# Another order for the head of a transformer-layer kernel: x turned by token tiles, and half of chunk 0 of the modulation behind four tiles of x

## What is computed

```python
c_act = silu(c)
mod = (c_act @ w_ada + b_ada)                  # 6144 columns: 12 chunks of 512
sh_m, sc_m, g_m, sh_f, sc_f, g_f = split(mod, 6)
u = layer_norm(x) * (1 + sc_m) + sh_m          # needs chunks 0, 1 (shift) and 2, 3 (scale)
z = u @ w_in                                   # 5120 columns: blocks of 128
# ... then pooling, chunked attention, a convolution, gates, projections,
# layer_norm, and an MLP (squared ReLU) with a second layer_norm
```

## Time and profile before

| | us |
|---|---|
| median of 3 runs | 1433.06 (1431.15 to 1433.45) |
| the profiled execution | 1431.08 |
| its span in the profile | 1429.3 |
| first matmul of the projections | 44.69 |
| first matmul of queries, keys and values | 122.37 |

### The profile page before, as it was taken

The page is one execution under the profiler, slowest core; times in us unless marked ns, Lnnn a source line. Parts: engine busy times, 40 slices in busy tenths (PEclk is TensorE's granted clock), DMA queues, the critical chain, the costliest instruction groups (busy, mean ns, idle before and its releaser), DMA issues.

```text
span 1429.3 us, 17335 instructions
## 1 busy us (share of the span) xinstructions
PE 1401.4 (98%) x6554; PEld 1150.8 (81%) x6554; DVE 965.6 (68%) x1334; ACT 634.6 (44%) x902; POOL 420.1 (29%) x453
## 2 busy tenths in 40 slices
PE   6999999999999999999999999999999999999996
PEld 1788788888878888888888888888888888888885
DVE  3877677776579955365668797565665746447687
ACT  3412577787541224111616774433445535343251
POOL 1005356556556000000024317434444200001215
PEclk9999999999999999999999999999999999999998
DMA  9883454665565322762632455444445978466361
GB/s 347 276 292 120 133 171 154 184 182 159 162 218 171 112 90 77 245 191 90 199 126 89 160 181 195 143 146 155 162 155 207 302 257 301 169 222 235 111 228 59
DMA packets 159035, 256.42 MB, mean 179 GB/s; under 512 B 11304, under 2 KB 81374, under 8 KB 158952
## 3 DMA queue, kind: packets, MB, share of 16 engines
q1 hardware_dynamic: 144104, 204.97, 42.9%
q0 software_dynamic: 14848, 50.34, 10.5%
HBM read 182.36 MB, written 68.71 MB: 176 GB/s over the span
## 4 chain that ended last, share of the span: by engine, by line
PE 83%; DVE 9%; DMA 2%; ACT 2%; issue 2%; SPq 1%; POOL 0%; DVEq 0%; ACTq 0%; POOLq 0%
PE ps L1977 22%; PE ps L1979 22%; PE ps L1978 22%; PE ps L2105 10%; PE ps L2145 2%; PE ps L2155 2%; PE ps L2170 2%; DVE bn L1330 1%; DMA mid<-in_x_dram 1%; DVE mid L1710 1%; DMA t_raw<-u_scratch 1%; DVE part_lo L1834 1%; DVE partial L1381 1%; DVE mix_tmp L1703 1%; PE ps L2044 1%
## 5 line engine op out<-in xcount | busy, mean ns | idle before, releaser
L1977 PE MATMUL ps<-act_hi,w_hi 128*128 128x512 f32 (+1 forms) x496 | 192.6, 388 | 0.4 <-DVE w_lo L1841 0.4
L1979 PE MATMUL ps<-act_hi,w_lo 128*128 128x512 f32 (+1 forms) x496 | 190.2, 384 | 0.0
L1978 PE MATMUL ps<-act_lo,w_hi 128*128 128x512 f32 (+1 forms) x496 | 190.0, 383 | 0.0
L1834 DVE TENSOR_TENSOR part_lo<-k_raw,part_hi 128x1024 fp32r<-128x1024 f32 x112 | 146.5, 1338 | 56.1 <-ACT part_hi L897 53.4
L1978 PE MATMUL ps<-part_lo,part_hi 128*128 128x512 f32 x448 | 174.3, 389 | 0.0
L1977 PE MATMUL ps<-part_hi 128*128 128x512 f32 x448 | 174.3, 389 | 0.0
L1979 PE MATMUL ps<-part_hi,part_lo 128*128 128x512 f32 x448 | 174.3, 389 | 0.0
L897 ACT ACTIVATE part_hi<-k_raw 128x1024 fp32r<-128x1024 f32 x112 | 116.4, 1059 | 110.6 <-DMA k_raw<-tw_scratch 48.9
L1324 DVE TENSOR_TENSOR w_lo<-w_raw,w_hi 128x1024 fp32r<-128x1024 f32 x52 | 68.5, 1316 | 68.4 <-ACT w_hi L897 68.3
L1977 PEld LDWEIGHTS ps<-act_hi,w_hi 128*128 128x128 f32 x496 | 93.4, 188 | 19.2 <-issue 0.7
L1978 PEld LDWEIGHTS ps<-act_lo,w_hi 128*128 128x128 f32 x496 | 93.5, 188 | 18.5 <-issue 1.0
(11 more groups left out here) (249 smaller groups left out, 3168.7 us busy)
## 6 DMA issues: line engine op xcount, KB each, us to landing
k_raw<-h_scratch SPq DMA_DIRECT2D x112, 256.0 KB, 4.5
ada<-in_w_ada_dram SPq DMA_DIRECT2D x11, 2048.0 KB, 9.4
w_raw<-in_w_in_dram SPq DMA_DIRECT2D x42, 512.0 KB, 4.5
tw_rows<-in_w_ff_dram POOLq DMA_DIRECT2D x64, 256.0 KB, 4.1
tw_scratch<-tw_sum POOLq DMA_DIRECT2D x32, 512.0 KB, 3.4
h_scratch<-h_sum POOLq DMA_DIRECT2D x64, 256.0 KB, 2.8
k_raw<-tw_scratch SPq DMA_DIRECT2D x64, 256.0 KB, 5.5
pair_raw<-in_w_ff_dram SPq DMA_DIRECT2D x13, 1024.0 KB, 6.1
```

The costliest lines, as they stand in the source:

```text
L1834: nc.vector.tensor_tensor(part_lo[s][:, :, :], k_raw[rs][:, :, :], f(part_hi[s][:, :, :]), ALU.subtract)\
L1977: nc.tensor.matmul(out, sh, mh, start=first, stop=False)
L1978: nc.tensor.matmul(out, sh, ml, start=False, stop=False)
L1979: return nc.tensor.matmul(out, sl, mh, start=False, stop=last)
```

## The change

The head is written anew up to the end of block 5; behind it nothing but the numbering of semaphores differs (some are merged, and the last tile's normalisation has one of its own).

- **Loads.** Chunk 0 comes in two halves with x tiles 0 to 3 between them, chunk 2 in two halves with tiles 4 and 5 between, then tiles 6 and 7, block 0, chunk 1, block 1, chunk 3, block 2 (waiting for `cut_lo(0)`), the biases, chunk 4 (waiting for DVE's chunk 1), block 3, and so on.
- **Chunk 1** goes from TensorE to DVE (`N_DIRECT` 2). Its columns are made by `row_columns(1)` out of `partial`.
- **Transposes** go by token tiles: eight transposes of one tile as soon as it is normalised, between the half chunks on TensorE. ACT copies each turned tile from PSUM to a new buffer `x_t` in SBUF (DVE the last one). ACT's modulation then reads `x_t`, and no longer waits for transposes.
- **act_hi** is cut by ACT instead of DVE, step 0 apart.
- **Products.** The steps of blocks 0, 1 and 2 are interleaved, with a third pair of buffers for block 2 in the place of normalised x. First steps 0 to 3 of blocks 0 and 1, then half of chunk 3, then steps 0 to 3 of block 2, then the columns of chunks 1 and 3, and then steps 4 to 7 of the three blocks. Blocks 3, 4 and 5 follow whole.

```diff
-N_DIRECT = 3
+N_DIRECT = 2
...
+            load_ada_half(0, 0)
+            load_x(range(4))
+            load_ada_half(0, 1)
...
+            load_ada_half(2, 0)
+            load_x(range(4, 6))
+            load_ada_half(2, 1)
+            load_x(range(6, ST))
+            load_block(0)
             load_ada(1)
-            load_x(range(5, ST))
-            load_block(0)
+            load_block(1)
             load_ada(3)
-            load_block(1)
...
+            def modulate_x(k):
                 if k >= 2:
                     act.wait_ge(u_lo_done, k - 1)
-                act.wait_ge(z_done, k + 1)
-                nc.scalar.activation(u_tmp[k % 2][:, :], banks(2 * (k % 2)), ACT.Identity, bias=mod[:, k:k + 1],
-                                     scale=mod[:, KT + k:KT + k + 1]).then_inc(u_tmp_done, 1)
+                nc.scalar.activation(u_tmp[k % 2][:, :], x_t[:, k, :], ACT.Identity, bias=mod[:, k:k + 1],
+                                     scale=mod[:, KT + k:KT + k + 1]).then_inc(u_step, 1)
+                if k >= 1:
+                    act.wait_ge(u_step, 2 * k)
+                    copy(act_hi[:, k, :], u_tmp[k % 2][:, :]).then_inc(u_step, 1)
...
+            act.wait_ge(mod_done, 1)
+            act.wait_ge(x_copied, ST)
+            for k in range(3):
+                modulate_x(k)
+            cut_hi(1)
+            modulate_x(3)
+            cut_hi(2)
+            save_ada_row(3)
+            act.wait_ge(mod_done, 2)
+            for k in range(4, KT):
+                modulate_x(k)
...
+            mixer_columns(0)
+            dve.wait_ge(z_done, ST)
+            nc.vector.tensor_copy(x_t[:, :, (ST - 1) * P:ST * P], tile_banks(ST - 1)).then_inc(x_copied, 1)
+            cut_lo(0)
+            cut_u_lo(0)
+            cut_u_lo(1)
+            cut_lo(1)
+            cut_u_lo(2)
+            start_chunk(1)
+            cut_u_lo(3)
+            end_chunk(1)
+            cut_lo(2)
+            ada_chunk(3)
+            mixer_columns(1)
+            cut_u_lo(4)
+            start_chunk(4)
+            for k in range(5, KT):
+                cut_u_lo(k)
+            end_chunk(4)
+            cut_lo(3)
...
             pe.wait_ge(head_sb_done, 2)
+            row_chunk(0, 0)
+            transpose_x(0)
+            transpose_x(1)
+            row_chunk(0, 1).then_inc(head_ps_done, 1)
+            transpose_x(2)
+            transpose_x(3)
...
+            row_chunk(2, 0)
+            transpose_x(4)
             row_columns(0)
+            transpose_x(5)
+            row_chunk(2, 1).then_inc(head_ps_done, 1)
+            transpose_x(6)
             row_columns(2)
+            transpose_x(7)
...
+            pe.wait_ge(w_lo_done, 1)
+            for k in range(2):
+                rows_part(0, k)
+            pe.wait_ge(w_lo_done, 2)
+            for k in range(2):
+                rows_part(1, k)
+            for n in range(2):
+                for k in range(2, 4):
+                    rows_part(n, k)
+            pe.wait_ge(mod_done, 1)
+            row_chunk(3, 0).then_inc(head_ps_done, 1)
+            pe.wait_ge(w_lo_done, 3)
+            for k in range(4):
+                rows_part(2, k)
+            row_columns(1)
+            row_columns(3)
+            for k in range(4, 6):
+                for n in (1, 0, 2):
+                    rows_part(n, k)
+            for n in (1, 0, 2):
+                for k in range(6, KT):
+                    rows_part(n, k)
```

More of the change, by code:

```diff
@@ L94, in trunk_layer @@
     act_lo = at("act_lo", [P, KT, SEQ], f32r, 32 * KB)
+    x_t = at("x_t", [P, KT, SEQ], f32, 32 * KB)
     mid = at("mid", [P, KT, SEQ], f32, 64 * KB)
@@ L338, in block_used @@
             if n < N_P1:
-                return z_done, 8 + n + 1
+                return z_done, ST + P1_END[n]
             if n < N_G:
@@ L920, in save_ada_row, with save_tile @@
             def save_ada_row(i):
-                act.wait_ge(head_ps_done, (1, 5, 4, 6)[i])
+                act.wait_ge(head_ps_done, {0: 1, 2: 4, 3: 5}[i])
                 copy(ada_row[i], ps[0:1, ADA_BANKS[i], :]).then_inc(head_sb_done, 1)
[L924 to L928, removed]
+            def save_tile(i):
+                act.wait_ge(z_done, i + 1)
+                copy(x_t[:, :, i * P:(i + 1) * P], tile_banks(i)).then_inc(x_copied, 1)
@@ L929, in _ @@
+            for i in range(0, ST, 2):
+                take_root(i, i)
+                take_root(i + 1, i + 1)
+                norm(i, i, mid[:, i, :])
+                if i + 1 < ST - 1:
+                    norm(i + 1, i + 1, mid[:, i + 1, :])
                 if i == 2:
                     save_ada_row(0)
-                elif i == 4:
+                if i == ST - 2:
                     save_ada_row(2)
[L933 to L941, removed]
+                    cut_hi(0)
+                    save_tile(i)
+                else:
+                    save_tile(i)
+                    save_tile(i + 1)
@@ new lines, in _ @@
+            act.wait_ge(mod_done, 1)
[9 more added lines that the diff above has]
+                modulate_x(k)
+            cut_hi(3)
+            for n in (0, 2, 3, 4, 5):
+                act.wait_ge(z_done, ST + P1_END[n])
+                src = banks(P1_BANKS[n])
@@ L1345, in _ @@
             dve.wait_ge(head_sb_done, 2)
[L1346 to L1351, removed]
+            for i in range(0, ST, 2):
+                for t in (i, i + 1):
+                    dve.wait_ge(x_in[t], 16)
+                    stats(mid[:, t, :], t)
+                for t in (i, i + 1):
+                    scale_bias(t, t)
+                if i == 4:
+                    dve.wait_ge(head_ps_done, 3)
+                    nc.vector.tensor_copy(cols[:, 0:ROWS_A], ps[:, 7, PIECE:PIECE + ROWS_A])
+                    nc.vector.tensor_copy(cols[:, ROWS_A:ROWS_A + ROWS_C], ps[:, 7, PIECE + P:PIECE + P + ROWS_C])\
+                        .then_inc(cols_done, 1)
             dve.wait_ge(norm_ready, ST)
             nc.vector.tensor_scalar(mid[:, ST - 1, :], mid[:, ST - 1, :], rstd[:, ST - 1:ST], neg_mean[:, ST - 1:ST],
-                                    ALU.mult, ALU.add).then_inc(normed, 1)
+                                    ALU.mult, ALU.add).then_inc(norm_end, 1)
             def ada_chunk(i):
@@ L1409, in mixer_columns, with cut_u_lo @@
                 nc.vector.tensor_scalar_add(scale, scale, 1.0).then_inc(mod_done, 1)
[L1411 to L1418, removed]
+            def cut_u_lo(k):
+                if k == 0:
+                    dve.wait_ge(u_step, 1)
+                    link(nc.vector.tensor_copy(act_hi[:, k, :], u_tmp[k % 2][:, :]))
+                else:
+                    dve.wait_ge(u_step, 2 * k + 1)
                 nc.vector.tensor_tensor(act_lo[:, k, :], u_tmp[k % 2][:, :], f(act_hi[:, k, :]), ALU.subtract)\
                     .then_inc(u_lo_done, 1)
[L1421 to L1429, removed]
+            mixer_columns(0)
[18 more added lines that the diff above has]
+            cut_lo(3)
+            dve.wait_ge(small_in, SMALL_BIASES)
+            nc.vector.tensor_copy(rel_ext[:, 2 * REL_CLIP:768],
+                                  rel_ext[:, 2 * REL_CLIP - 1:2 * REL_CLIP]
+                                  .to_broadcast([HEADS, 768 - 2 * REL_CLIP])).then_inc(rel_done, 1)
             def conv_tap(n):
@@ L1450, in pool_means, with take_glu @@
                                                    op0=ALU.mult, op1=ALU.subtract).then_inc(pooled_done, 1)
[L1452 to L1466, removed]
+            def take_glu(t):
+                n = 2 * t + 1
+                dve.wait_ge(z_done, ST + P1_END[n])
+                dve.wait_ge(glu_sig_done, t + 1)
+                dve.wait_ge(consts_done, 7)
+                nc.vector.tensor_tensor(h_pad[:, t, PAD:PAD + SEQ], banks(P1_BANKS[n]), glu_gate[:, :], ALU.mult)\
+                    .then_inc(glu_done, 1)
+            start_chunk(5)
+            take_glu(0)
+            end_chunk(5)
+            cut_lo(4)
+            ada_chunk(6)
+            take_glu(1)
+            cut_lo(5)
+            gate_chunk(4)
+            gate_chunk(5)
+            ada_chunk(7)
+            ada_chunk(8)
+            cut_lo(6)
+            ada_chunk(9)
+            cut_lo(7)
+            pool_means(0)
             def cut_lo_after(pair, r):
@@ L2027, in reduce_chunk, with transpose_x @@
                 ins.then_inc(reduced, 1)
-            pe.wait_ge(head_sb_done, 2)
-            row_chunk(0)
-            pe.wait_ge(small_in, 16 * 8)
-            nc.tensor.transpose(ps[:, 4, 0:ROWS_A], rows_a[:, :], ident[0:ROWS_A, 0:ROWS_A]).then_inc(head_ps_done, 1)
-            nc.tensor.transpose(ps[:, 5, 0:ROWS_C], rows_c[:, :], ident[0:ROWS_C, 0:ROWS_C]).then_inc(head_ps_done, 1)
-            row_chunk(2)
+            def transpose_x(i):
+                if i < ST - 1:
+                    pe.wait_ge(normed, i + 1)
+                else:
+                    pe.wait_ge(norm_end, 1)
+                if i >= 2:
+                    pe.wait_ge(x_copied, i - 1)
```

(26 more changed lines are left out.)

209 lines of the change are left out of this document (111 added, 98 removed).

## The result

The changed kernel takes 1433.56 us (median of 20; 1432.21 to 1435.84) beside 1431.43 us of the kernel before on the same chips: a ratio of 1.0015, 95% interval 1.0009 to 1.0021. That is 2.1 us more. Its profiled execution was the longest of the twenty, 1435.84 us with a span of 1434.1.

What follows compares the result with a forecast made beforehand. PE, 98% busy, was taken as the bound: 75.6 us of its work, 7.2 idle and 1.4 of clock behind a first product 5.1 us earlier, plus 0.6 for hops, gave +2.2 us, median 1435.3; range 1430.0 to 1440.0.

Steps and rivals of the forecast that it cites:

- The bound and the instant: PE, busy 98%, bounds the kernel; a shift of the queries' start, 122.37 us before, goes through to the end.
- 0.6 for hops: Estimate added for the dozen hops between engines from 34.8 to 70.4 us, most between engines with queues of their own.
- six sets of transposes: Counted in PE's 77.7 us from 44.69 us to the queries before the change: 0.85 each, 5.1 us.
- When the data come: Loads in the head at 0.38 MB per us: chunk 0's first half at 8.3 us, its second half at 16.6.
- The first product: After tile 7's copy and step 0's modulation and cuts, it starts at 39.6 us, 5.1 us earlier than before.
- The two short waits: PE, paced by DVE's list, waits 1.9 us for block 1's low part and another 1.0 before 49.5 us.
- The stall ahead of step 4: Columns end at 66.1 us, step 4 is ready at 70.4; PE idles 4.3 us with nothing else able to run.
- The clock behind it: After columns and idle time PE restarts at half clock, costing between nothing and 1.7 us; 1.4 taken.
- The stall isn't paid: Rival, faster: ready work covers the wait for the columns, 4.3 + 1.4 go, shift -4.1, about 1429; chance 0.12.
- Half clock in the head: Rival, slower: clock falls ahead of chunk 2's second half, 1.7 to 3.5 lost, about 1438; chance 0.30.
- The change doesn't do what it says: Rival: chunk 0's second half lands with x; worth nothing, as PE is at the transposes until 16.7 us; no chance given.
- The Trainium skill's rule: Rule against the change: full clock doesn't engage for transposes, making the sum 4.2 us higher; the prediction followed the trace instead.

Runs made afterwards that it cites:

- The spare matmuls: The changed kernel with 18 spare matmuls of 128x512 on PE between the last transposes and the first product: 1433.29 us, ratio 1.0007 to the kernel before.
- four tiles and two: The changed kernel with two tiles of x instead of four between the halves of chunk 0: 1433.41 us, ratio 1.0014 to the kernel before.
- the spare matmuls: The changed kernel with 17 spare matmuls of 128x512 on PE in its idle stretch behind the columns: 1432.79 us, ratio 1.0004 to the kernel before.

## Why the prediction was right, step by step

- **The bound and the instant.** The queries' start was forecast at 124.6 (124.0 and 0.6 for hops); it was 125.4 in one profile and 124.1 in the other. The median moved by 2.1 us; 2.2 were forecast. That a shift goes through to the end unchanged held only roughly: the remainder was 1306.3 to 1308.7 us in the ten profiles, a difference as large as the whole effect, and no profile shows a median execution. So the sign and the rough size come from the mechanism, the agreement to 0.1 us is luck. The absolute forecast, 1435.3, was 1.7 us too high, nearly all of it because the kernel before took 1431.43 on these chips and not 1433.06.
- **One miscount without effect.** Between 44.69 us and the queries the prediction counts six sets of transposes; the kernel before has five there, so 0.85 us more of the 77.7 is left unexplained. The 1.7 us for the half clock stand all the same, as half of the stretch from 52.2 to 55.6 us, and the forecast's own sum has no transposes behind 34.8 us.
- **When the data come.** Chunk 0's first half ended PE's wait at 7.2 us, 1.1 sooner than worked out. It was worth little: PE's chain began at 15.6 instead of 16.7 and ended at 34.5 instead of 34.8, as the six sets of transposes took 0.9 to 1.1 us each instead of 0.85.
- **The first product**: 39.6 forecast, 39.2 and 39.1 measured. Tile 7's copy out of PSUM on DVE took 1.23, by the upper of the two bounds that I had given it.
- **The two short waits**, 1.9 and 1.0 us, were right in their cause and didn't show as such: PE ran at half clock there and the waits shrank to under 1 us. The spare matmuls brought back 1.52 and 0.79. I had put no half clock at that place; as DVE paces it, its price is nothing.
- **The stall ahead of step 4**: 4.3 forecast, 4.15 measured, ended by the low part of step 4, with the columns ending at 65.7 (66.1 forecast). Moving the columns took it away, and the time with it; this step carries the forecast, and it is shown.
- **The clock behind it** was the term that I mis-sized: 1.4 us, as between nothing and the 1.7 of before. It cost 3.1 in one execution and 1.9 in the other, so the upper end was too low. The 0.6 for hops, which I had added as an estimate, wasn't there: the first product came 0.4 to 0.5 us early and step 4 0.5 us early (69.9 instead of 70.4). These errors offset each other in part, and that they did is luck.
- **The rivals.** *The stall isn't paid* would have given 1429; that needed the columns "about 4 us before PE's order allows", and with another order it came true (1428.1 and 1429.3). *Half clock in the head* came true only with chunk 0 loaded whole. *The change doesn't do what it says*: four tiles and two are indeed the same.
- **The Trainium skill's rule** on transposes ("TensorE: Matmul & The Clock Gate", "Part 4: PE-mode transpose"), that the full clock doesn't engage for them, is again not what the trace shows: sixteen took 3.67 us where the granted clock was 0.50 and 1.97 where it was 1.00. They run at whichever clock is granted; whether transposes alone would keep it up, no run here shows.

## What to carry to other kernels

When work is brought forward, look for the first result that everything behind needs, and see whether the engine that makes it still has other work queued behind it; if that other work is put ahead of the result, the time won is waited away (here 5.5 us won, 4.15 lost to idle time and 2 to 3 to the clock after it). Swapping two pieces of one engine's list can be worth more than the rewrite that it is part of: the swap alone turned 0.15% slower into 0.2% faster. And compare instants at which both kernels start the same work, rather than spans of single profiles.

## What the runs showed of the hardware that was not expected

- The half-clock stretch behind the same stall lasted to 76.1 us in one execution of one kernel and into the 74th us in another; this alone moved the queries by 1.2 us.
- Half clock came behind columns in one piece without any idle time (from 59.9 us on with the columns ahead of block 2, from about 65.6 on, as the columns ended, ahead of the spare matmuls), with PE busy by the record throughout. In the one profile with the same columns set between products and a half chunk it didn't come.
- A half-clock stretch on an engine that another one paces was free here, and covered waits that a faster clock shows: 1.52 us of wait appeared when the clock was kept up.
- One wait of 1.7 us, the same in all ten profiles, was followed by half clock in three of them (17 matmuls in the 5 us behind it) and by full clock in seven (26 matmuls).
